# Letting accumulating DMA transfers make the sums of a scan's two rotations

## The reference

```python
u = x @ w_u                                  # 256 tokens x 1024
bu_re, bu_im = u @ B_re, u @ B_im            # 64 groups x 64 states
b = (cf_re + i cf_im) * (bu_re + i bu_im)
s[t] = (ab_re + i ab_im) * s[t-1] + b[t]     # complex, over the 256 tokens
y = s_re @ C_re - s_im @ C_im + D_skip * u
```

```python
back:     d_re = b_re * c + b_im * s         d_im = b_im * c - b_re * s
scan:     r[t] = mag * r[t-1] + d[t]         (for re and for im)
forward:  s_re = r_re * c - r_im * s         s_im = r_re * s + r_im * c
```

## Time and profile before

| | |
|---|---|
| median of 3 runs | 3322.17 us (3321.44 to 3323.22) |
| the profiled execution, its time | 3322.21 us |
| the profiled execution, its span | 3320.3 us |
| PE busy, share of the span | 95% |
| DVE busy | 61% |
| ACT busy | 46% |
| POOL busy | 2% |
| the 8 chunks of the scan | from 2753 to 3099 us |

### The profile page before, as it was taken

How to read it: one execution, slowest core, us unless ns; L and a number is a source line. 1 busy time by engine, 2 the same in 40 slices (tenths; PEclk the granted TensorE clock), 3 DMA queues, 4 the chain that set the end, 5 groups by cost and what they waited for, 6 DMA issues and landing times.

```text
span 3320.3 us, 47412 instructions
## 1 busy us (share of the span) xinstructions
PE 3140.2 (95%) x17370; PEld 2725.1 (82%) x17370; DVE 2021.3 (61%) x2350; ACT 1538.3 (46%) x1975; POOL 59.3 (2%) x99
## 2 busy tenths in 40 slices
PE   8999898999999998989989999999997998999999
PEld 7798777888888887987877888888885888989997
DVE  5567755555555555676655555555556557888664
ACT  5554545544444444545455444444444455544443
POOL 0000000000000000000000000000001000000000
PEclk9999999999999999999999999999998999999999
DMA  6645363655555555544554555555553433444555
GB/s 238 221 167 175 134 211 119 207 189 188 190 187 189 187 189 171 178 147 152 180 169 154 196 184 190 189 190 189 184 189 114 164 111 129 156 146 153 169 178 180
DMA packets 159835, 577.01 MB, mean 174 GB/s; under 512 B 17504, under 2 KB 20240, under 8 KB 158544
## 3 DMA queue, kind: packets, MB, share of 16 engines
q1 hardware_dynamic: 151936, 549.52, 49.6%
q10 hardware_dynamic: 5616, 13.51, 1.2%
q0 software_dynamic: 2144, 12.02, 1.0%
HBM read 568.43 MB, written 6.55 MB: 173 GB/s over the span
## 4 chain that ended last, share of the span: by engine, by line
PE 74%; DVE 11%; ACT 5%; issue 4%; DVEq 3%; DMA 1%; ACTq 1%; POOL 1%; POOLq 0%; SPq 0%
PE acc L624 19%; PE acc L626 19%; PE acc L625 19%; PE acc L632 4%; PE acc L634 4%; PE acc L635 4%; DVE lo L1482 3%; PE tp L643 1%; DVE sr L2098 1%; ACT hi L1020 1%; PE tp L676 1%; ACT lg L1102 1%; DVEq L2076 0%; PE tp L774 0%; ACT ze L1353 0%
## 5 line engine op out<-in xcount | busy, mean ns | idle before, releaser
L1482 DVE TENSOR_TENSOR lo<-raw,hi 128x1024 fp32r<-128x1024 f32 x1040 | 1263.4, 1223 | 943.5 <-ACT hi L1020 934.7
L1020 ACT ACTIVATE hi<-raw 128x1024 fp32r<-128x1024 f32 x1040 | 1093.9, 1058 | 1273.6 <-PE acc L626 970.4
L624 PE MATMUL acc<-hi,xh 128*128 128x512 f32 (+2 forms) x2272 | 883.8, 389 | 6.7 <-DVE lo L1482 3.7
L625 PE MATMUL acc<-lo,xh 128*128 128x512 f32 (+2 forms) x2272 | 875.8, 385 | 0.0
L626 PE MATMUL acc<-hi,xl 128*128 128x512 f32 (+2 forms) x2272 | 875.5, 385 | 0.0
L632 PE MATMUL acc<-xh,hi 128*128 128x256 f32 x1664 | 487.3, 293 | 35.9 <-DVE lo L1482 35.5
L624 PEld LDWEIGHTS acc<-hi,xh 128*128 128x128 f32 x2272 | 428.5, 189 | 94.7 <-issue 6.6
L626 PEld LDWEIGHTS acc<-hi,xl 128*128 128x128 f32 x2272 | 428.4, 189 | 85.1
L625 PEld LDWEIGHTS acc<-lo,xh 128*128 128x128 f32 x2272 | 428.7, 189 | 82.5
L634 PE MATMUL acc<-xl,hi 128*128 128x256 f32 x1664 | 476.3, 286 | 0.0
L635 PE MATMUL acc<-xh,lo 128*128 128x256 f32 x1664 | 476.0, 286 | 0.0
(11 more groups left out here) (366 smaller groups left out, 2629.8 us busy)
## 6 DMA issues: line engine op xcount, KB each, us to landing
raw<-in_stream SPq DMA_DIRECT2D x1040, 512.0 KB, 3.4
gpost<-in_post_g POOLq DMA_DIRECT2D x6, 1024.0 KB, 5.1
bpad<-in_b_pad ACTq DMA_DIRECT2D x8, 512.0 KB, 5.1
row<-in_rows POOLq DMA_DIRECT2D x3, 896.0 KB, 8.7
toep_scratch<-toep ACTq DMA_DIRECT2D x1, 2304.0 KB, 7.9
y<-in_mem SPq DMA_DIRECT2D x4, 512.0 KB, 8.4
h<-in_x ACTq DMA_DIRECT2D x4, 512.0 KB, 5.8
mem_scratch<-memkv ACTq DMA_DIRECT2D x1, 2048.0 KB, 6.6
```

The costliest lines, as they stand in the source:

```text
L624: nc.tensor.matmul(o, ah, hi[s][:, k, 0:g.width], start=first, stop=False)
L625: nc.tensor.matmul(o, ah, lo[s][:, k, 0:g.width], start=False, stop=False)
L1020: nc.scalar.activation(hi[s][:, :, :], raw[s][:, :, :], ACT.Copy).then_inc(hi_done, 1)
L1482: nc.vector.tensor_tensor(lo[s][:, :, :], raw[s][:, :, :], hi[s][:, :, :].bitcast(F32), ALU.subtract).then_inc(split_done, 1)
```

## The change

The two products that used to be added on VectorE are written to `srs` (the two `sr` tiles as one tensor), with their sign, and the two they are added to are in `sds` (the two `sd` tiles as one). VectorE signals, and GpSimd issues one DMA transfer that adds all of `srs` (128 partitions x 2048 floats, 1 MB) onto `sds`. That happens twice in each chunk: after `back` (signal `backed`, the transfer signals `summed`, for which the scan waits) and after `forward` (signal `turned_back`, the transfer signals `states`, for which `outputs` waits). `join` is gone, `st` is gone, `scan` moves from place 2.8 to 3.2 and `forward` from 4 to 4.1. ScalarE's `turns` waits for `turned_back` instead of `states`.

```diff
-        scan = [(0, "inputs", c), (1, "back", c), (2, "maps", c), (2.8, "scan", c), (4, "forward", c), (5, "join", c),
+        scan = [(0, "inputs", c), (1, "back", c), (2, "maps", c), (3.2, "scan", c), (4.1, "forward", c),
                 (7.2, "outputs", c), (7.9, "skip", c)]
...
-        sd = [at_offset(f"sd{n}", m_at + 16384 + 4096 * n, [P, 4, T]) for n in range(2)]
+        sds = at_offset("sds", m_at + 16384, [P, 2, 4, T])
+        sd = [sds[:, n, :, :] for n in range(2)]
...
-        sr = [at_offset(f"sr{n}", r_at + 4096 * n, [P, 4, T]) for n in range(2)]
-        st = at_offset("st", r_at + 8192, [P, 4, T])
+        srs = at_offset("srs", r_at, [P, 2, 4, T])
+        sr = [srs[:, n, :, :] for n in range(2)]
...
-                    pe.wait_ge(states, c + 1)
+                    pe.wait_ge(states, 16 * (c + 1))
...
-                        act.wait_ge(states, c)
+                        act.wait_ge(turned_back, c)
...
-                    nc.vector.tensor_tensor(sr[0][:, :, :], o[:, :, :], rots[:, :, :], ALU.mult)\
+                    nc.vector.scalar_tensor_tensor(sr[1][:, :, :], o[:, :, :], -1.0, rots[:, :, :], ALU.mult, ALU.mult)\
                       .then_inc(tp_read[STP[f"s{c}_re"] % 2], 1)
                     o = see_turn(dve, pos, STP[f"s{c}_im"])
                     nc.vector.tensor_tensor(sd[1][:, :, :], o[:, :, :], rotc[:, :, :], ALU.mult)
-                    nc.vector.tensor_tensor(st[:, :, :], o[:, :, :], rots[:, :, :], ALU.mult)\
+                    nc.vector.tensor_tensor(sr[0][:, :, :], o[:, :, :], rots[:, :, :], ALU.mult)\
                       .then_inc(tp_read[STP[f"s{c}_im"] % 2], 1)
-                    dve.drain()
-                    nc.vector.tensor_tensor(sd[0][:, :, :], sd[0][:, :, :], st[:, :, :], ALU.add)
-                    nc.vector.tensor_tensor(sd[1][:, :, :], sd[1][:, :, :], sr[0][:, :, :], ALU.subtract)
+                    dve.drain().then_inc(backed, 1)
...
                 elif step == "scan":
 
                     c = at[0]
-                    dve.drain()
+                    dve.wait_ge(summed, 16 * (c + 1))
...
-                    nc.vector.tensor_tensor(st[:, :, :], sr[1][:, :, :], rots[:, :, :], ALU.mult)
+                    dve.drain()
+                    nc.vector.scalar_tensor_tensor(sr[0][:, :, :], sr[1][:, :, :], -1.0, rots[:, :, :], ALU.mult, ALU.mult)
                     dve.drain()
                     nc.vector.tensor_tensor(sr[1][:, :, :], sr[1][:, :, :], rotc[:, :, :], ALU.mult)
-                elif step == "join":
-                    c = at[0]
-                    dve.drain()
-                    nc.vector.tensor_tensor(sd[0][:, :, :], sd[0][:, :, :], st[:, :, :], ALU.subtract)
-                    nc.vector.tensor_tensor(sd[1][:, :, :], sd[1][:, :, :], sr[1][:, :, :], ALU.add).then_inc(states, 1)
+                    dve.drain().then_inc(turned_back, 1)
...
+            for c in range(NCT):
+                hold(pool, backed, c + 1, passed)
+                pool.dma_start(flat(sds), flat(srs), accum_op=ALU.add).then_inc(summed, 16)
+                hold(pool, turned_back, c + 1, passed)
+                pool.dma_start(flat(sds), flat(srs), accum_op=ALU.add).then_inc(states, 16)
```

More of the change, by code:

```diff
@@ L479, in build @@
         turned = sem("turned")
+        backed = sem("backed")
+        summed = sem("summed")
+        turned_back = sem("turned_back")
         states = sem("states")
```

## The result

The changed kernel takes 3356.2 us (3352.6 to 3357.6), the kernel before 3322.7 in the same comparison: 1.0101 times as long, 95% interval 1.0089 to 1.0114. It is slower by 33.5 us where 10.5 were forecast. The profiled execution has a span of 3355.5 us.

A forecast was written before the change was run, and what follows sets the result against it. VectorE was taken to hold TensorE up in the scan's stretch. At D = 8.5: +6.3 us for seven chunks, +1.6 for the last, +2.6 for the clock, +10.5 on 3322.2, predicted 3332.5 us; 8-in-10 range 3302 to 3378.

The forecast's parts named there:

- the forecast's own case: Both added transfers: each takes 7.8 to 9.2 us, giving 3318 to 3348 us; chance 0.44.
- D: Each added transfer: GpSimd's issue, movement of 1 MB and the signal; 8.5 us taken.
- a slow transfer: Rival at both transfers: 10 us or more each, 3369 us at 10.2 and +83 at 11.9; chance 0.20.
- a starving stream: Rival: weight loads queue behind the transfers, holding TensorE up 1 us for each of sixteen; some 3354 us; chance 0.06.
- The price is the transfer's time, and adding about doubles what the bytes take.: Both transfers: a sum that took VectorE 2.3 us now takes a transfer's time, 8.5 us, since both operands are read.
- A chain that closes once in each chunk takes the cost on, at 2 D.: From `back` over scan, `forward` and `outputs` to the next `back`, with both transfers: at least 28.4 + 2 D us a chunk.
- The pitch at D = 8.5.: Time of one chunk of the scan: 45.4 us, 0.9 more than the 44.5 before, seven times: +6.3 us.
- the fixed part of the chain, 28.4 us: A chunk's chain without transfers: 15.4 us for `back`, scan, one `lo` and `forward`, plus 13 from `outputs` to `back`.
- The leg from `outputs` to `back`, 13.9 in the mean.: TensorE's `outputs`, units and `inputs`, then a `hi` and a `lo`: 13.9 us mean, taken as 13 as VectorE's backlog shrinks.
- The clock as a third of a microsecond on each microsecond of waiting, added at the end, 2.6 us.: TensorE's clock in the scan's stretch: 8 us more of waiting lowers it, adding 2.6 us to the total.
- TensorE's waits move from `lo` to `states`.: Scan's stretch: TensorE waits for the second transfer in most chunks; its waits for `lo` fall below 26.6 us.
- The quick transfer, 3310 us at D = 7.1 and 3300 at 5.1.: Rival at both transfers: below 7.6 us each, so faster; half the some 43 us winnable given back at 5.1; chance 0.30.

The follow-up runs named there:

- first transfer only: Changed kernel with only the sums behind `back` made by a transfer, those of `forward` on VectorE as before: 3331.5 us, 1.0034.
- second only: Changed kernel with only the sums behind `forward` made by a transfer, those of `back` on VectorE as before: 3352.6 us, 1.0094.
- copy: Changed kernel with both transfers copying `srs` onto `sds` instead of adding, sums left out of the computation: 3306.0 us, 0.9954.
- half the bytes: Changed kernel with each transfer adding only the first of two pairs, 512 KB for 1 MB, other sums left out: 3308.6 us, 0.9962.
- after, pause filled: Changed kernel with ten matmuls on constants ahead of TensorE's wait for the transfer in five chunks: 3348.3 us, 1.0089.
- second only, filled: Kernel with only the transfer behind `forward`, plus ten matmuls on constants ahead of TensorE's wait in five chunks: 3333.3 us, 1.0041.
- after, outputs at 8.0: Changed kernel with `outputs` moved from place 7.2 to 8.0, just ahead of the next chunk's `inputs`: 3329.1 us, 1.0023.
- second only, 8.0: Kernel with only the transfer behind `forward`, with `outputs` at place 8.0 instead of 7.2: 3315.9 us, 0.9984.
- before, 8.0: Kernel before the change with only the place of `outputs` changed, 8.0 for 7.2: 3332.4 us, 1.0029.
- sums shared: Changed kernel with each transfer adding the first pair (512 KB) while VectorE adds the second pair, whole computation done: 3319.9 us, 0.9998.
- mixed: Changed kernel: behind `back` transfer and VectorE add one pair each; behind `forward` the transfer adds both, `outputs` at 8.0: 3321.7 us, 0.9999.

## Why the prediction was right, and where its size was off

The legs of all kernels in us, and TensorE's waits for the second transfer and for `lo` (2740 to 3160 us). The traces of the copy and of the three kernels with `outputs` at 8.0 are of executions 2 to 6 us shorter than the medians.

| kernel | median | pitch | back to scan | scan to last product | last product to outputs | outputs to next back | wait, transfer | wait, lo |
|---|---|---|---|---|---|---|---|---|
| before | 3322.7 | 44.5 | 12.1 | 10.4 | 7.2 | 15.0 | 0 | 26.6 |
| after | 3356.2 | 48.9 | 14.1 | 9.9 | 10.8 | 14.1 | 26.8 | 26.0 |
| first transfer only | 3331.5 | 45.6 | 14.0 | 9.7 | 6.7 | 15.6 | 0 | 30.9 |
| second only | 3352.6 | 49.0 | 12.1 | 10.6 | 11.3 | 14.8 | 33.2 | 19.9 |
| copy | 3306.0 | 42.4 | 11.6 | 9.9 | 7.8 | 13.2 | 4.6 | 16.7 |
| half the bytes | 3308.6 | 43.1 | 11.9 | 9.9 | 8.0 | 13.4 | 8.3 | 16.6 |
| after, pause filled | 3348.3 | 47.8 | 14.1 | 9.9 | 11.2 | 12.6 | 4.5 | 30.6 |
| second only, filled | 3333.3 | 46.4 | 12.1 | 10.6 | 11.0 | 12.5 | 7.2 | 21.4 |
| after, outputs at 8.0 | 3329.1 | 45.3 | 14.2 | 9.9 | 12.0 | 9.0 | 3.7 | 35.1 |
| second only, 8.0 | 3315.9 | 43.9 | 12.2 | 10.6 | 11.9 | 9.0 | 3.9 | 24.6 |
| before, 8.0 | 3332.4 | 46.0 | 12.2 | 10.4 | 13.6 | 9.4 | 0 | 37.5 |
| sums shared | 3319.9 | 44.2 | 12.2 | 10.0 | 9.0 | 13.1 | 0 | 29.6 |
| mixed | 3321.7 | 44.8 | 11.4 | 10.3 | 12.0 | 10.9 | 2.1 | 23.1 |

The direction, the transfer's time and the chain were right. The size was not: 33.5 us for 10.5 (added to 3322.2 that makes 3332.7; 3332.5 was written). The measured time lies inside the wide range (3302 to 3378), but outside the range of the forecast's own case (3318 to 3348), although D came out inside that case, at 8.7. With D = 8.7 the sum gives 3337 us; 19 us are missing. What the wide range had above 3348 was meant for a slow transfer and a starving stream, and neither happened. That 3356 also lies near the 3354 of the starving stream is chance.

- *The price is the transfer's time, and adding about doubles what the bytes take.* Right. 8.5 us were forecast from the doubled row, 8.7 measured, 5.2 for the copy. That it is the second read which costs is argued.
- *A chain that closes once in each chunk takes the cost on, at 2 D.* Right in kind: half the bytes took 5.8 us from the pitch for 2 x 3.0 of D, the copy 6.5 for 2 x 3.5, and with `outputs` moved the time followed the legs. With one transfer away it did so for the first transfer and not for the second.
- *The pitch at D = 8.5.* 45.4 was forecast, 48.9 measured, and the fixed part of the chain, 28.4 us, is the step that was too small: 3.5 us, seven times, are 24.5 us of the 23.7 between forecast and measurement. By its terms: 0.9 and 1.0 us from the two ways over a transfer, since D was counted from GpSimd's issue, and VectorE's `drain` and the signal lie ahead of it, 0.6 to 0.65 us, and the landing was 0.2 longer; 0.35 from the second `drain` of `forward` and one more `lo` in one chunk; 1.1 from the leg from `outputs` to `back`, 14.1 for the 13 that I took.
- *The leg from `outputs` to `back`, 13.9 in the mean.* That was the mean of three of seven; all seven of the kernel before give 15.0. The 13 that was taken is about what the leg measures with the pauses filled (12.6 and 12.5), so the 1.1 us are the clock's doing. The 4.4 us from the end of the last product to `outputs` were one chunk's too; the mean of eight is 5.9.
- *The clock as a third of a microsecond on each microsecond of waiting, added at the end, 2.6 us.* This was the wrong place for it. TensorE's pause ahead of `outputs` slows the very matmuls that the chain waits for. With the pauses filled the kernel with only the second transfer is 19 us quicker; for the changed kernel it is 8 us by the medians, within what the two intervals leave open. Where TensorE waits at the end of the chain, it pays twice: for the wait and for the slower matmuls behind it.
- *TensorE's waits move from `lo` to `states`.* Wrong. They came on top. 34.5 us less work of VectorE took 0.6 us off the waits for `lo`. All but one of them end at the same two places as most did before, with the first `lo` behind the scans and the first behind `forward`, and VectorE stood 19.5 us at the scan ahead of them. With a quick transfer (copy and half) the same four sums less do take 10 us off.
- *The quick transfer, 3310 us at D = 7.1 and 3300 at 5.1.* The copy (D = 5.2) gave 3306.0, half the bytes (5.7) 3308.6, both without the full sums. The give-back for VectorE's bursts, half of the prize, was a little low there: 16 us were won for the 22 forecast.
- *The weight stream starves.* Loads did come later, and ScalarE waited 31.3 us for them after 21.2, but that is not the loss: the kernel with only the second transfer waited 15.4 and lost 30.9 us, and eight transfers beside the kernel before cost nothing that can be told. In the mixed kernel two late loads did reach TensorE, 3.6 and 3.1 us.
- *VectorE waits at the scan for D less 5, 3 us a chunk.* 19.5 us in eight chunks, 2.4 in each.

What stays open: why the costs of the two transfers don't add up, and what would take VectorE's row of scans and products off `lo`. Neither was tried alone.

## What to carry to other kernels

Before work is handed from a busy engine to a transfer, draw the chain from a buffer's write to its next write: a transfer on it costs its whole time from the last product to landing, here 9.3 us for 1 MB added. A copy of the same bytes landed in 5.2 us for the 8.7, so price an adding transfer by itself. Look at who waits at its end: here it was TensorE, and the first matmuls behind its pauses ran at the lower clock. Moving independent units of work into the pause brought the loss from 33.5 to 7.9 us. Work taken off an engine brings nothing where it doesn't shorten the row of instructions that others wait behind: with two of four sums gone from each chunk, the row ahead of the late `lo` was no shorter than before, and neither was the program.

## What the runs showed of the hardware that was not expected

- An accumulating transfer of 1 MB from SBUF to SBUF landed in 8.7 us, a copy of the same bytes in 5.2, 512 KB accumulated in 4.7 to 5.7.
- GpSimd's issue takes 0.84 to 0.95 us for an accumulating one, 0.53 (once 0.62) for the copy of the same bytes from SBUF to SBUF, and 0.61 to 0.63 for a copy of 1 MB from HBM.
- With 50 needless matmuls ahead of TensorE's waits, the kernel with only the second transfer finished 19 us sooner; the median of the 128 matmuls behind the waits went from 632 to 379 ns.
- Eight accumulating transfers beside the chain, 8 MB, changed the time by a ratio of 1.0005 (at most 1.0014), while ScalarE's longest wait for a load of 512 KB went from 3.5 to 9.0 us.
